# TensorE's moving columns and accumulator columns in pairs of 16-column lines, moving tensors 256 bytes off the weights

## The reference, cut to what matters

```python
def swiglu_ffn(h, w_up, w_down):
    a, b = jnp.split(h @ w_up, 2, axis=-1)
    return (jax.nn.silu(a) * b) @ w_down
...
    for l in range(DEPTH):                                   # first block
        x = x + 0.5 * swiglu_ffn(rmsnorm(x, ffn1_norm[l]), ffn1_w_up[l], ffn1_w_down[l])
        x = x + mixer(rmsnorm(x, mix_norm[l]), ...)           # attention, 31-tap convolution, gates
        x = x + 0.5 * swiglu_ffn(rmsnorm(x, ffn2_norm[l]), ffn2_w_up[l], ffn2_w_down[l])
        x = rmsnorm(x, final_norm[l])
...
    for l in range(DEPTH):                                   # second block
        ...                                                  # Fourier mixing and windowed attention
        up = dwconv_centred(h @ w_up[l], conv_w[l], conv_b[l])
        gate, val = up[..., :D_FF_2], up[..., D_FF_2:]
        x = x + (jax.nn.silu(gate) * val) @ w_down[l]
```

## Time and profile before

| | us |
|---|---|
| median of 3 runs | 1942.4 |
| lowest, highest | 1942.34, 1946.62 |
| the profiled execution | 1953.66 |
| its span, first to last instruction | 1951.7 |

### The profile page before, as it was taken

The page is one execution under the profiler, slowest core; times in us unless marked ns, Lnnn a source line. Parts: engine busy times, 40 slices in busy tenths (PEclk is TensorE's granted clock), DMA queues, the critical chain, the costliest instruction groups (busy, mean ns, idle before and its releaser), DMA issues.

```text
span 1951.7 us, 38913 instructions
## 1 busy us (share of the span) xinstructions
PE 1906.9 (98%) x15852; PEld 1837.7 (94%) x15852; DVE 1467.1 (75%) x2147; ACT 1105.0 (57%) x1414; POOL 41.7 (2%) x52
## 2 busy tenths in 40 slices
PE   7999999999999999999999999999999999999998
PEld 7999898899999999998997999999889999889998
DVE  5555799987765585568999877656888778878777
ACT  5444666676544464446676765444656556556554
POOL 0000011000000000000110000000000000000000
PEclk9999999999999999999999999999999999999999
DMA  6556599634665545556996346555335554335554
GB/s 256 200 178 222 191 295 285 172 105 145 209 215 192 192 173 191 177 209 215 281 263 184 90 150 231 199 193 180 125 118 188 191 193 166 130 123 190 192 192 152
DMA packets 62732, 368.59 MB, mean 189 GB/s; under 512 B 8096, under 2 KB 8352, under 8 KB 25888
## 3 DMA queue, kind: packets, MB, share of 16 engines
q1 hardware_dynamic: 54704, 339.37, 50.0%
q0 software_dynamic: 6912, 25.17, 7.2%
q10 hardware_dynamic: 1008, 2.51, 0.3%
HBM read 359.68 MB, written 1.05 MB: 185 GB/s over the span
## 4 chain that ended last, share of the span: by engine, by line
PE 74%; DVE 17%; ACT 4%; DMA 3%; issue 2%; SPq 0%; DVEq 0%; ACTq 0%
PE bank L447 23%; PE bank L448 22%; PE bank L449 22%; DVE lo L1659 5%; DVE cv L1912 5%; ACT hi L1078 2%; DVE zt L1875 1%; DMA zt<-zt 1%; PE bank L629 1%; DMA lo<-in_w 1%; PE bank L656 1%; ACT n_hi L1140 1%; PE bank L642 1%; PE bank L614 1%; DVE qk L1877 1%
## 5 line engine op out<-in xcount | busy, mean ns | idle before, releaser
L1659 DVE TENSOR_TENSOR lo<-raw,hi 128x2048 fp32r<-128x2048 f32 (+1 forms) x336 | 663.9, 1977 | 197.6 <-ACT hi L1078 196.9
L1078 ACT ACTIVATE hi<-raw 128x2048 fp32r<-128x2048 f32 (+1 forms) x336 | 598.7, 1784 | 103.5 <-PE bank L449 89.6
L447 PE MATMUL bank<-n_hi,hi 128*128 128x256 f32 x2256 | 635.7, 282 | 21.0 <-DVE lo L1939 12.2
L448 PE MATMUL bank<-n_lo,hi 128*128 128x256 f32 x2256 | 629.0, 279 | 0.0
L449 PE MATMUL bank<-n_hi,lo 128*128 128x256 f32 x2256 | 628.9, 279 | 0.0
L447 PEld LDWEIGHTS bank<-n_hi,hi 128*128 128x128 f32 x2256 | 427.5, 189 | 27.0 <-DVE lo L1939 12.2
L448 PEld LDWEIGHTS bank<-n_lo,hi 128*128 128x128 f32 x2256 | 424.6, 188 | 1.3 <-issue 1.0
L449 PEld LDWEIGHTS bank<-n_hi,lo 128*128 128x128 f32 x2256 | 425.8, 189 | 0.0
L447 PE MATMUL bank<-h_hi,hi 128*128 128x256 f32 x1152 | 330.8, 287 | 6.3 <-DVE h_lo L1663 4.0
L448 PE MATMUL bank<-h_lo,hi 128*128 128x256 f32 x1152 | 321.4, 279 | 0.0
L449 PE MATMUL bank<-h_hi,lo 128*128 128x256 f32 x1152 | 321.3, 279 | 0.0
(11 more groups left out here) (271 smaller groups left out, 2325.7 us busy)
## 6 DMA issues: line engine op xcount, KB each, us to landing
raw<-in_w SPq DMA_DIRECT2D x286, 1024.0 KB, 4.9
raw<-in_w SPq DMA_DIRECT2D x53, 512.0 KB, 3.8
lo<-in_w POOLq DMA_DIRECT2D x48, 512.0 KB, 8.8
zt<-zt SPq DMA_DIRECT2D x96, 64.0 KB, 6.7
bv<-in_bv SPq DMA_DIRECT2D x2, 768.0 KB, 6.2
spread<-in_spread SPq DMA_DIRECT2D x2, 768.0 KB, 8.0
x<-in_x ACTq DMA_DIRECT2D x4, 256.0 KB, 10.1
out_x<-sq SPq DMA_DIRECT2D x1, 1024.0 KB, 3.9
```

The source lines that it names most:

```text
L447: mm(out, w_hi, a_hi, start=start, stop=False, skip_group_check=True)
L448: mm(out, w_hi, a_lo, start=False, stop=False, skip_group_check=True)
L1078: fn(hi[:, s, 0:w], raw[:, s, 0:w], ACT.Copy).then_inc(sem["hi"], 1)
L1659: v.tensor_tensor(lo[:, s, 0:w], raw[:, s, 0:w], hi[:, s, 0:w].bitcast(F32), ALU.subtract)\
```

## The change

`mm3` rearranges what it gets before it issues its three matmuls. Where the last dimension is 256 columns, the operand is seen as 2 halves (`h`) of 8 lines (`j`) of 16 columns (`i`), and walked line by line with the halves inside: columns 0 to 15, 128 to 143, 16 to 31, 144 to 159, and so on. The two halves are 128 columns, 512 bytes, apart. The moving operand is read in this order and the accumulator written in the same, so each column lands where it did. Operands of another width (512 and 128 columns) stay as they were. The weights are loaded as before. The number of matmuls, their order and all waits stay; nothing is moved on any engine.

The padding in `build` is changed so that `x`, `h_hi`, `h_lo`, `sq` and all from `qk` on begin 256 instead of 192 bytes past a multiple of 512 from the weights; `const` and the small tensors stay where they were relative to the weights, and `cv`, `gate`, `bv`, `spread`, `zgsq` go from 128 to 192.

```diff
+LINE = 16
...
-    state["at"] += 192
+    state["at"] += 256
     x = sb("x", [P, KT, S], F32)
     h_hi = sb("h_hi", [P, KT, S], F32R)
     h_lo = sb("h_lo", [P, KT, S], F32R)
     sq = sb("sq", [P, KT, S], F32)
-    state["at"] += 320
+    state["at"] += 256
     const = sb("const", [P, C["mask1"]], F32)
...
+    state["at"] += 64
     at_a = state["at"]
     qk = sb("qk", [P, 24, S], F32)
...
+        def by_lines(t):
+
+            if t.shape[-1] != S:
+                return t
+            return t.rearrange("p (h j i) -> p j h i", h=2, i=LINE)
+
         def mm3(out, w_hi, w_lo, a_hi, a_lo, start=False):
 
+            out, a_hi, a_lo = by_lines(out), by_lines(a_hi), by_lines(a_lo)
             mm(out, w_hi, a_hi, start=start, stop=False, skip_group_check=True)
             mm(out, w_hi, a_lo, start=False, stop=False, skip_group_check=True)
             return mm(out, w_lo, a_hi, start=False, stop=True, skip_group_check=True)
```

## The result

The changed kernel takes 2003.3 us (1998.0 to 2005.2, four runs) against 1943.2 for the kernel before beside it: a ratio of 1.0287, with a 95% interval of 1.0241 to 1.0332. It is 60 us slower; 1877 was forecast, in 1864 to 1946.

The account below looks back on a forecast made before the run. PE, busy 98% of the span, was taken to bound the kernel at two paces, 113 and 118 ns. Savings of 51.5 us in feed-forward bodies plus 19 us elsewhere, 70.5 us, gave 1877 us, in 1864 to 1946.

Parts of the forecast that it names:

- The reads meet: In each `mm3` matmul the moving read passes the weight read once, costing 4 or 8.6 ns at two phases.
- The rival that nothing happens: Independent read ports for moving operand and weights make column order worth nothing: 1942 us, in 1936 to 1948; chance 0.12.
- Made of parts that repeat every 512 bytes: If memory repeats so, the twice as fast moving read must pass the weight read once per matmul, wherever they start.
- (2): Moving base at 256: both halves of a pair stay 256 bytes from the weights, so each 256-column `mm3` matmul takes 109 ns.
- Both go in step ... nothing is passed any more: Walked in pairs, the moving read advances 64 bytes in 13.3 ns, the weight read in 13.4, so they never meet.
- 109 ns when the two don't hurt each other: Pace taken for 256-column `mm3` matmuls without meeting, from 109.7 ns between transposes and 106.7 ns for the columns.
- only the 118 ns pace goes: Rival: the 113 ns pace stays; 18 us saved in the bodies, about 5 elsewhere; 1919 us, in 1910 to 1926; chance 0.18.
- The sum: Saving 8.6 or 4.1 ns per matmul: 51.5 us in six feed-forward bodies plus 19 us elsewhere, 70.5 us in all.
- Its reckoning of the path: Some 1200 matmuls where DVE is full gain nothing; of 28.4 us for 4580 others outside the bodies, two thirds count.
- Each new run costs: Rival: cutting 256 columns into 16 runs, in read and accumulator, costs two periods each: 122.3 ns, 2032 us; chance 0.12.
- In step, but on top of each other: Rival: a lagging or reversed weight read meets the moving read longer or as often: 126 ns, 10.8 over today, 2080 us; 0.06.
- 512-column products: Matmuls of 512 columns, 231.7 ns each before, 18 ns over 213.3; a sign of being right was staying near 230 ns.

Follow-up runs that it names:

- small kernels: Five kernels without the reference's work, running blocks of 48 matmuls of one form with other engines nearly still; no 256-column form came under 113.3 ns.
- last small kernel: Such blocks with moving columns read downwards, or every 2nd, 4th or 8th weight column, against one run upwards; pairs downwards 113.3 to 120.7 ns.

## Why the prediction was wrong, point by point

- **What bounds the kernel: right.** PE sets the time, at one of two paces that it keeps for a stage, and the start picks it. The small kernels have both paces with all other engines still.
- **The reads meet: right for one run.** Distance alone takes the pace from 113.3 to 120.0 with the form unchanged, wherever the two lie. The rival that nothing happens, from independent reads, falls with it.
- **"Made of parts that repeat every 512 bytes": the first step that failed.** They repeat every 256. No row showed 512; it is the unit in which this kernel counts its padding and its weight tiles. So (2), "both halves 256 bytes from the weights, the farthest possible", put them at distance 0. This term was to be a gain and is worth +60.7 us by itself.
- **"Both go in step ... nothing is passed any more": the second.** Taken alone at the good base, the walk costs +62.4 us. Read upwards in pairs, the moving operand comes every 120.0 ns at every base and even over standing weights. Going in step isn't worth anything either where it is tried without pairs: 117.7 to 121.2 ns for one run over every second weight column. In the prediction only the distance of two reads had a price; that the order in which the moving read goes through the parts has one too was not in it. Whether that is a price of the order itself or of its direction against the weights' read stays open, since the same pairs downwards reach 113.3.
- **"109 ns when the two don't hurt each other": the third.** The floor came from transposes with 128 columns, 109.7 ns. A load with 128 moving float32r columns paces at 111.7, and the best of 256 columns is the 113.3 that the kernel already had in half its stages. The formula that the prediction set beside it, columns / 2.4 GHz plus about 2.5 ns, is given in that section of the Trainium skill (TensorE: Matmul & The Clock Gate, Back-to-back issue gap) for a single matmul by itself, not for a stream in which each has its load; its 109.2 ns is 4.1 under all that was seen here. With everything else right there was nothing to gain where the 113 ns pace ran; even the rival "only the 118 ns pace goes" was an upper bound, some 23 us.
- **The sum.** In place of -8.6 and -4.1 ns on each matmul stand +2.2 and +6.4 (157.9/1315 is 120.1 and 172.1/1418, less its wait, 120.3). The 13,970 products go from a mean of 115.2 to 120.0, 67 us if PE paced them all; the medians differ by 60. Two side sums were off without weight: by the prediction's own counts 106.7 ns in place of 109 would take 26 us more, not at most 18, and 109.2 ns would make the sum 2 us smaller, not 1. Its reckoning of the path did well: the two DVE stretches lose 1.8 and 1.0 us of the 6 that their 1200 products would make, as the earlier trace rows said for the other sign.
- **The rivals.** "Each new run costs" had the sign and the nearest time, but the wrong mechanism: 16 runs in the accumulator cost nothing, 16 runs in order nothing at 0 and 128, and the base alone costs all of the loss with no run cut. The timing alone would have passed for it: (120.0 - 109)/16 is 0.7 ns a run, between its one and two periods of 0.42. Only the kernels with one part each, and then the forms, told it apart. The Trainium skill's sentence that a non-contiguous pattern slows matmuls (PSUM — Partial Sum Buffer, Specifications (TRN2)) isn't borne out here for the accumulator, at 5.73 us a block to 5.72. "In step, but on top of each other" came closest in mechanism: at 256 the moving columns do lie on top of the weights, and weights read from the last column to the first are what the reads downwards hint at. But the meeting costs as much when nothing is in step (the base alone), and its price was 10.8 ns over the mean where 4.8 is measured. Its 6% was too little: the choice between far and near hung on the period, which no row gave, and the two periods should have had a chance each.
- **512-column products**: forecast at 230 ns, measured 226.7 ns (nine distances from 214.80 to 216.84 us), 5 under the earlier trace rows. Their walk was left as it was, so the layout or the start made them faster; which of the two wasn't tried.

```profile
214.80 0.39 PE L458 MATMUL bank<-hi,n_lo 128*128 128x512 f32 x1
...
216.84 0.39 PE L458 MATMUL bank<-hi,n_lo 128*128 128x512 f32 x1
```

**What stays open.** Why pairs are slow upwards and not downwards, why the wrong order costs the time of two 16-column lines (120.0 - 106.7 = 13.3 ns = 2 x 6.67) and the right one that of one (6.6), what in the start decides between 113.3 and 117.8, and in which order weights are read. No kernel here beats the one before.

## What to carry to other kernels

Where two reads of one engine may meet, measure the period and the price of each distance in a stream of that one matmul before the layout or the walk is changed; two paces of one form, told apart by the start alone, can be a sign of addresses, as here, but don't say which are good. Floors are to be taken from the same form: here the better of the two paces that the kernel already had was the floor. And when a change has two parts, each of which is argued from the same unmeasured number, the chances of a gain are those of that number.

## What the runs showed of the hardware

- A float32r matmul with its own 128-column load paces at 113.3 ns at best for 256 columns, and at 120.0 at worst for one run. The distance of moving columns from weights modulo 256 bytes decides, and at some distances the start too, at 2.4 GHz.
- In the accumulator 16 pieces of 16 columns cost nothing (5.73 us a block to 5.72).
- A narrower matmul may be slower: 252 columns 120.0 ns, 256 columns 113.3, one block each at the same distance.
- A read that stays in one 64-byte line is not cheap but dear: 121.2 to 122.3 ns with standing weights (line 79 above), 120.0 to 122.3 with ordinary ones.
- A weight operand with a step of 4 columns, 16 bytes, takes twice the time (mostly 233.3 ns a matmul), with a step of 2 it does not (117.7 to 124.1). A block of the former, in the timeline of the last small kernel:

```profile
343.09 11.48 PE L87 MATMUL bank<-mb,wa 128*128 128x256 f32 x48 [0.33 <-DVE tmp L120]
```
